# Rotary embedding of queries and keys done inside the projection's own PSUM bank

## What is computed

```python
def apply_rope(t, cos, sin):
    t1, t2 = jnp.split(t, 2, axis=-1)
    rot = jnp.concatenate([-t2, t1], axis=-1)
    return (t * cos + rot * sin).astype(t.dtype)
...
q, k, v = jnp.split(h @ w_in, 3, axis=-1)
q = apply_rope(q.reshape(Bn, S, C_HEADS, HEAD_DIM), cos, sin)
k = apply_rope(k.reshape(Bn, S, C_HEADS, HEAD_DIM), cos, sin)
```

## Time and profile before

| what | value |
|---|---|
| median of three executions | 1525.03 us |
| the profiled execution | 1525.93 us, span 1523.9 us |
| TensorE (PE) busy | 1357.9 us, 89% |
| VectorE (DVE) busy | 1044.0 us, 69% |
| ScalarE (ACT) busy | 598.5 us, 39% |
| mean granted TensorE clock | 0.952 of full |

### The profile page before, as it was taken

How to read it: one execution, slowest core, us unless ns; L and a number is a source line. 1 busy time by engine, 2 the same in 40 slices (tenths; PEclk the granted TensorE clock), 3 DMA queues, 4 the chain that set the end, 5 groups by cost and what they waited for, 6 DMA issues and landing times.

```text
span 1523.9 us, 22456 instructions
## 1 busy us (share of the span) xinstructions
PE 1357.9 (89%) x8718; PEld 1206.9 (79%) x8718; DVE 1044.0 (69%) x1478; ACT 598.5 (39%) x800; POOL 2.9 (0%) x5
## 2 busy tenths in 40 slices
PE   3875889999898788999959997999996899999997
PEld 3753679999797677999849986899986676899996
DVE  6979788777777757766676785755568645575554
ACT  1424333343344424333345322534336453353332
POOL 0000000000000000000000000000000000000000
PEclk9898889999899998999979998999999999999999
DMA  9653438877375334655516430455452310454540
GB/s 357 262 184 106 153 116 328 315 268 257 122 266 185 132 111 181 231 215 191 203 48 224 139 111 28 166 193 191 171 189 107 135 63 29 166 208 175 188 160 28
DMA packets 45841, 262.90 MB, mean 173 GB/s; under 512 B 5191, under 2 KB 6855, under 8 KB 21066
## 3 DMA queue, kind: packets, MB, share of 16 engines
q1 hardware_dynamic: 32672, 216.88, 39.2%
q10 hardware_dynamic: 13102, 45.09, 8.5%
HBM read 260.90 MB, written 1.05 MB: 172 GB/s over the span
## 4 chain that ended last, share of the span: by engine, by line
PE 73%; DVE 17%; ACT 4%; issue 3%; DMA 2%; ACTq 0%; DVEq 0%; SPq 0%
PE banks L530 21%; PE banks L531 21%; PE banks L532 21%; DVE w_lo L1496 3%; DMA A<-ada_w 2%; PE banks L737 2%; PE banks L998 2%; PE banks L694 1%; ACT A L1053 1%; ACT w_hi L1037 1%; DVE A L1516 1%; DVE hT_lo L1485 1%; PE banks L640 1%; DVE A L1505 1%; DVE mx L1602 1%
## 5 line engine op out<-in xcount | busy, mean ns | idle before, releaser
L1496 DVE TENSOR_TENSOR w_lo<-raw,w_hi 128x2048 fp32r<-128x2048 f32 x193 | 439.8, 2287 | 160.4 <-ACT w_hi L1037 158.1
L1037 ACT ACTIVATE w_hi<-raw 128x2048 fp32r<-128x2048 f32 x193 | 368.8, 1913 | 246.4 <-PE banks L532 211.6
L530 PE MATMUL banks<-hT_hi,w_hi 128*128 128x256 f32 x1432 | 414.0, 289 | 7.6 <-DVE hT_lo L1485 3.3
L532 PE MATMUL banks<-hT_hi,w_lo 128*128 128x256 f32 x1432 | 410.2, 286 | 0.0
L531 PE MATMUL banks<-hT_lo,w_hi 128*128 128x256 f32 x1432 | 410.1, 286 | 0.0
L530 PEld LDWEIGHTS banks<-hT_hi,w_hi 128*128 128x128 f32 x1432 | 280.2, 196 | 13.5 <-issue 7.4
L531 PEld LDWEIGHTS banks<-hT_lo,w_hi 128*128 128x128 f32 x1432 | 280.1, 196 | 3.3 <-issue 1.0
L532 PEld LDWEIGHTS banks<-hT_hi,w_lo 128*128 128x128 f32 x1432 | 279.7, 195 | 0.0
L530 PE MATMUL banks<-w_hi,R 128*128 128x512 f32 (+1 forms) x592 | 231.2, 390 | 3.9 <-DVE R L1485 3.6
L531 PE MATMUL banks<-w_lo,R 128*128 128x512 f32 (+1 forms) x592 | 229.3, 387 | 0.0
L532 PE MATMUL banks<-w_hi,R 128*128 128x512 f32 (+1 forms) x592 | 228.7, 386 | 0.0
(11 more groups left out here) (221 smaller groups left out, 1329.1 us busy)
## 6 DMA issues: line engine op xcount, KB each, us to landing
raw<-stream SPq DMA_DIRECT2D x193, 1024.0 KB, 4.8
A<-ada_w ACTq DMA_DIRECT2D x73, 512.0 KB, 5.4
A<-ada_w SPq DMA_DIRECT2D x16, 512.0 KB, 9.8
A<-ln_g ACTq DMA_DIRECT2D x4, 512.0 KB, 4.0
A<-ln_b ACTq DMA_DIRECT2D x4, 512.0 KB, 5.5
A<-ada_w SPq DMA_DIRECT2D x1, 1536.0 KB
A<-x_t SPq DMA_DIRECT2D x2, 512.0 KB, 12.4
X<-ada_w SPq DMA_DIRECT2D x1, 1024.0 KB
```

Source lines behind the costliest of these rows:

```text
L530: pe.matmul(o, lh, rh, start=start, stop=False, skip_group_check=True)
L532: return pe.matmul(o, ll, rh, start=False, stop=stop, skip_group_check=True)
L1037: act.activation(w_hi[:, s, :], raw[:, s, :], ACT.Copy).then_inc(hi_done, 1)
L1496: v.tensor_tensor(w_lo[:, s, :], raw[:, s, :], w_hi[:, s, :], ALU.subtract).then_inc(lo_done, 1)
```

## The change

The projection stays in its bank until it is rotated. VectorE reads the bank twice: once times sin, with the sign turned, into an SBUF buffer (a permutation swaps halves whose sines have opposite signs, so the product is taken before the swap), once times cos in place, written back into the bank. TensorE then multiplies the SBUF buffer by `perm` and accumulates into the same bank (`start=False`), and ScalarE copies the sum to where the rotated tile belongs, which now signals `roped`. The ScalarE copy thus moves from the `fill` step to the end of the `rope` step. Three banks, 2, 0 and 1, serve the rotations in turn, bank 6 the one of 256 columns; a bank is free again at `roped`. For rotations, the second 256 columns of a fill no longer start a group of their own.

```diff
+        def rope_bank(r):
+            return 6 if r == 16 else (2, 0, 1)[r % 3]
...
-                b = n["fill"] % 2
+                b = rope_bank(n["rope"]) if reader == "rope" else n["fill"] % 2
...
+                    if form == "Th":
+                        pe.wait_ge(y_read, n["y"])
...
-                                               k == 0, k == kts - 1)
+                                               k == 0 and not (a and reader == "rope"), k == kts - 1 and reader != "rope")
...
-                held[b] = ({"plain": fill_read, "rope": turn_f, "e": e_done}[key], n[key])
+                held[b] = ({"plain": fill_read, "rope": roped, "e": e_done}[key], n[key])
...
                     pe.wait_ge(turn_f, n["turn"] + 1)
-                    claim(2)
                     buf, w = a[0] + 512 * (n["turn"] % 2), a[3]
-                    pe.matmul(B[2][:, 0:w], perm[:, :], A[:, buf:buf + w], start=True, stop=True).then_inc(turn_ps, 1)
+                    pe.matmul(B[rope_bank(n["turn"])][:, 0:w], perm[:, :], A[:, buf:buf + w], start=False, stop=True,
+                              skip_group_check=True).then_inc(turn_ps, 1)
...
-                        if r >= 2:
-                            act.wait_ge(roped, r - 1)
-                        act.activation(A[:, dst + 512 * (r % 2):][:, 0:w], bank[:, 0:w], ACT.Copy).then_inc(turn_f, 1)
+                        pass
...
+                elif kind == "rope":
+                    dst, w = a[2], a[3]
+                    act.wait_ge(turn_ps, n["rope"] + 1)
+                    act.activation(A[:, dst:dst + w], B[rope_bank(n["rope"])][:, 0:w], ACT.Copy).then_inc(roped, 1)
...
-                    v.wait_ge(turn_f, r + 1)
+                    v.wait_ge(*filled[r])
...
+                    if r >= 2:
+                        v.wait_ge(turn_ps, r - 1)
...
-                    mark(v.tensor_tensor(shape(d), shape(f), cos, ALU.mult))
-                    v.wait_ge(turn_ps, r + 1)
-                    link(v.tensor_tensor(shape(tb), shape(B[2][:, 0:w]), sin, ALU.mult))
-                    v.tensor_tensor(d, d, tb, ALU.add).then_inc(roped, 1)
+                    v.scalar_tensor_tensor(out=shape(tb), in0=shape(ps), scalar=-1.0, in1=sin, op0=ALU.mult, op1=ALU.mult)
+                    v.tensor_tensor(shape(ps), shape(ps), cos, ALU.mult).then_inc(turn_f, 1)
```

More of the change, by code:

```diff
@@ L864, in _ @@
                     pe.wait_ge(turn_f, n["turn"] + 1)
-                    claim(2)
                     buf, w = a[0] + 512 * (n["turn"] % 2), a[3]
-                    pe.matmul(B[2][:, 0:w], perm[:, :], A[:, buf:buf + w], start=True, stop=True).then_inc(turn_ps, 1)
+                    pe.matmul(B[rope_bank(n["turn"])][:, 0:w], perm[:, :], A[:, buf:buf + w], start=False, stop=True,
+                              skip_group_check=True).then_inc(turn_ps, 1)
                     n["turn"] += 1
-                    held[2] = (roped, n["turn"])
                 elif kind == "turn2":
@@ L1213, in _ @@
                     u, part, parts, form, src, reader, dst = a
[L1214 to L1218, removed]
+                    n["part"] += part < parts - 1
+                    if reader != "rope":
+                        act.wait_ge(*((unit_done, u + 1) if part == parts - 1 else (fill_done, n["part"])))
                     bank = B[n["fill"] % 2]
@@ L1228, in _ @@
                     elif reader == "rope":
-                        w = 256 if form == "Th" else 512
-                        r = n["rope"]
-                        if r >= 2:
-                            act.wait_ge(roped, r - 1)
-                        act.activation(A[:, dst + 512 * (r % 2):][:, 0:w], bank[:, 0:w], ACT.Copy).then_inc(turn_f, 1)
-                        n["rope"] += 1
+                        pass
                     else:
@@ L1247, in _ @@
                         ahead(u)
+                elif kind == "rope":
+                    dst, w = a[2], a[3]
+                    act.wait_ge(turn_ps, n["rope"] + 1)
+                    act.activation(A[:, dst:dst + w], B[rope_bank(n["rope"])][:, 0:w], ACT.Copy).then_inc(roped, 1)
+                    n["rope"] += 1
                 elif kind == "turn2":
@@ L1422, in _ @@
         def _(v):
-            n = dict(step=0, plain=0, rope=0, pair=0, e=0, row=0, n=0, gates=0, x=0, y=0, sq=0, root=0, half=0, f=0, staged=0, u={})
+            n = dict(step=0, plain=0, rope=0, pair=0, e=0, row=0, n=0, gates=0, x=0, y=0, sq=0, root=0, half=0, f=0, staged=0, part=0, u={})
+            filled = []
             def link(ins):
@@ L1712, in _ @@
                     n["plain"] += reader == "plain"
+                    n["part"] += part < parts - 1
+                    if reader == "rope":
+                        filled.append((unit_done, u + 1) if part == parts - 1 else (fill_done, n["part"]))
                     if reader == "plain":
@@ L1751, in _ @@
                     tmp += 512 * (r % 2)
-                    d, f, tb = A[:, dst:dst + w], A[:, tmp:tmp + w], A[:, turned_at:turned_at + w]
+                    tb, ps = A[:, tmp:tmp + w], B[rope_bank(r)][:, 0:w]
                     v.wait_ge(pair_ready, n["pair"])
-                    mark(v.tensor_tensor(shape(d), shape(f), cos, ALU.mult))
-                    v.wait_ge(turn_ps, r + 1)
-                    link(v.tensor_tensor(shape(tb), shape(B[2][:, 0:w]), sin, ALU.mult))
-                    v.tensor_tensor(d, d, tb, ALU.add).then_inc(roped, 1)
+                    v.scalar_tensor_tensor(out=shape(tb), in0=shape(ps), scalar=-1.0, in1=sin, op0=ALU.mult, op1=ALU.mult)
+                    v.tensor_tensor(shape(ps), shape(ps), cos, ALU.mult).then_inc(turn_f, 1)
                 elif kind == "ada":
```

## The result

The change takes **1544.57 us** (median of four executions, 1543.03 to 1546.47) against 1525.75 us of the kernel before on the same chip: 1.2% slower, ratio 1.012 [1.0106, 1.0134], +18.8 us. The profiled execution took 1545.37 us, span 1543.6; its mean granted clock is 0.939, before it was 0.952.

What follows compares the result with a forecast made beforehand. VectorE was taken as full in AB, TensorE as the busier engine in C. Terms of -0.4 (AB), +3.2, +0.9, +1.8 (C) and +1.9 (MLA) sum to +7.4 us, forecasting 1533 us, range 1526 to 1538.5.

Steps and rivals of the forecast that it cites:

- The price of a bank write: VectorE's in-place product into a PSUM bank: taken as 0.69 us each, 1.3 us a pair.
- The waits: TensorE waits for the cos product, some 6 us before C's fill 2, 2.5 in MLA; score 5 waits for ScalarE's copy.
- AB, "-0.4": Mixer AB: earlier gate sums are mostly lost to new waits at later permutations, leaving a gain of 0.4 us.
- about 2.3: Mixer AB: cost in us of the permutation ahead of the first index products, now waiting for VectorE's sums and product pair.
- From there on VectorE is the bound: Mixer AB, from the first maxima (125.16) on: VectorE sets the pace, so the -0.4 us stays.
- C, the end: +1.8: End of mixer C: score 5 comes 1.4 us later, score 6 2.1, of which the maxima see 1.8; nothing absorbs it.
- C, the start, "+3.2": Start of mixer C: the first permutation waits for VectorE's products, delaying fill 2 and score 0; +3.2 us of 2.4 to 4.3.
- The steps between: Middle of mixer C: scores 2 and 4 wait for `w_hi` and a copy; +0.9 us together.
- MLA, "+1.9" of 1.3 to 3.5: Mixer MLA: the 256-column permutation waits for its products, delaying the fills and four big rotations; +1.9 us in total.
- Rival C: TensorE's clock falls in the new gaps of AB, C and MLA: 1538 us, chance 0.12.
- The MLP stretches unchanged: Stretches outside the three mixers: predicted to keep their length, as one sign of the forecast.
- rival D: VectorE's in-place product is dear (twice 0.69 us) or does not do what it says: 1541 us, chance 0.03.

## Why the prediction was right in kind and wrong in size

The step that failed is the price of TensorE's work behind the new waits. The places of the waits were foreseen, but AB and the end of C were added up as if TensorE's matmuls behind them kept their length. The runs show that work running slower: TensorE was busy 14.4 us longer with the same matmuls.

Stage by stage, in us against the profile of the kernel before, from the first `w_hi` and the five places named above. The last two columns are the change with its gaps filled (1531.26 us) and the kernel before filled at C's end (1523.56 us):

| stage | predicted | the change | gaps filled | before, C's end filled |
|---|---|---|---|---|
| up to the first `w_hi` | 0 | -1.1 | -1.7 | -0.9 |
| AB | -0.4 | +5.4 | +2.1 | +0.4 |
| up to C | 0 | -2.7 | -1.2 | -1.3 |
| C | +5.9 | +13.0 | +2.2 | -3.0 |
| up to MLA | 0 | +1.5 | -0.1 | +3.5 |
| MLA | +1.9 | +3.5 | +2.7 | 0.0 |
| sum | +7.4 | +19.6 | +4.1 | -1.3 |

The rows are rounded, and their spread between executions is as large as told above: the last column has +3.5 in a stretch that is the same in both kernels.

**The price of a bank write: right.** 0.69 us was taken, 690 ns measured, and 687 ns for the form with a scalar. The Trainium skill's 62 cycles for a PSUM source ("VectorE: DVE Perf Modes", section on the TRN2 errata) don't show in these rows either: 687 and 690 ns with a bank as a source, 692 ns without one.

**The waits: right in place.** Gate, permutation, the copy behind `w_hi`, score 5 waiting for the copy: all are in the trace. One reading was too simple: before the change, too, the permutation waited for VectorE, 9.1 us in all, for the sum of an earlier rotation. The mixers' waits for the product were foreseen at about 6 and 2.5 us, and measured at 5.0 (rotation 0 of C) and 5.5 (the 256 columns of MLA). The latter's products stood behind two `w_lo`.

**AB, "-0.4": failed.** I let the permutation behind the modulation sums cost "about 2.3", with its length of a second as at the full clock. It waited 4.63 us, then ran at half the clock, and so did the index products. The maxima came 2.3 us later than before where I had 0.4 earlier. Of these 2.7 us, 0.8 stood in the index sums of head 3 already (117.25, not 116.5); the last permutation and the scores behind it took 1.05 and 0.72 us longer than at the full clock. "From there on VectorE is the bound" failed too: 2.0 us more were lost from the maxima to the end of the stage, where the mean clock was 0.75 for 0.81 before. What TensorE and VectorE each have in these 2.0 us was not separated. With the gaps filled AB is at +2.1.

**"C, the end: +1.8": failed in the same way.** From score 4 (+7.7) to the `w_hi` after the attention (+14.6) it is 6.9 us. Score 5 gave the +1.4 that I had said, and score 6 +2.0 (I said 2.1, and let 1.8 count for the whole end). The other 3.6 us lie behind score 6, where I wrote that "nothing absorbs it", and had no term for its growth: 25 us at the lower clock.

**C, the start, "+3.2": low.** Score 0 moved by 6.5 us within the mixer and 1.8 came back at score 1, so +4.8; the bound was 4.3. The first permutation took 2.08 us for 1.02, and fill 2 behind it 8.0 us, where I had let it grow to 7.0 only. The steps between were +1.3, said +0.9.

**MLA, "+1.9" of 1.3 to 3.5: at its upper bound,** the one that I had given for a lower clock, or over it: with MLA alone changed the median rose by 5.4 us.

**Rival C was the truth, at twice its price and more.** I gave "the clock falls in the new gaps" 0.12 and 1538 us. Filling the gaps takes 13.3 us off the change, but only 2.6 us off the kernel before (there at C's end alone). Filled against filled, 1531.26 against 1523.56, the change costs 7.7 us, give or take 3. So some 8 of the 18.8 us are the order's and up to 11 the clock's; up to, since the gaps of the kernel before in AB and MLA were never filled, and may give something back too. My sum of 7.4 is near the order's share, but that is partly luck: the sum held small terms for the clock at C's start, and the stages differ in both directions. The Trainium skill, "TensorE: Matmul & The Clock Gate", section "HAM oscillation — how this bites in real kernels", describes a kernel whose waits bring the clock down again and again, so that it loses on the matmuls too; by that rule rival C deserved most of the chance. The trace agrees: 0.50 from 534 to 559.

"The MLP stretches unchanged" is neither borne out nor refuted. In the change's profile 2.7 us come back before C, but kernels whose rotations differ from before's only in C or MLA, or not at all, show -1.0 to -1.3 there too, and kernels with the change's AB show anything from -2.7 to +3.5.

One sum in the prediction doesn't come out: rival D's terms give 1533.3 + 8 x 0.7 = 1538.9, not 1541. Nothing hung on it.

The order can remove all of the loss (1525.33, then 1518.62), the filled gaps most of it (1531.26). They overlap, as a gap that is gone needs no filling; both together give 1514.0.

## What to carry to other kernels

When a step's producer moves to another in-order engine, go through that engine's list and move the step ahead of whatever waits for a DMA or serves a later stage; here this turned +18.8 us into -8.0. A wait on TensorE has two prices, its length and the slower matmuls behind it. In a chain where the engines take turns, price the second from rows of the same work at either clock. A form that looks worse in the old order may suit a better order that the old form does not, so judge it after the order is mended.

## What had not been expected of the hardware

Unread matmuls of 256 columns made a kernel faster by 13.3 us with its order untouched. And the same instructions in AB take different times from one execution to the next: in the change and in the three kernels that differ from it in the order of C alone, the place after AB's attention was at 189.59, 191.94, 193.00 and 190.31 us. Mixer C, unchanged, cost 13.0 us in one profile and 7.9 in another. A difference of 2 us in one stage of one profile shows nothing here, and one of 5 us little; the medians do.
